# Opening loads cut up and reordered, first low parts on GpSimd, spread product moved into the second gate product

## The reference

```python
def _rmsnorm(x, gain):
    xf = x.astype(jnp.float32)
    y = xf * lax.rsqrt(jnp.mean(xf * xf, axis=-1, keepdims=True) + RMS_EPS)
    return (y * gain.astype(jnp.float32)).astype(x.dtype)
...
    for l in range(DEPTH):
        x = x + 0.5 * swiglu(rmsnorm(x, ffn1_norm[l]), ffn1_w_gate[l], ffn1_w_up[l], ffn1_w_down[l])
```

## Time and profile before

| | us |
|---|---|
| median of 3 runs | 1238.55 (1238.48, 1238.55, 1239.64) |
| span of the profiled execution | 1237.2 |
| PE busy | 1220.2 |
| GpSimd busy | 777.1 |
| ScalarE busy | 617.8 |
| VectorE busy | 538.6 |

### The profile page before, as it was taken

How to read it: one execution, slowest core, us unless ns; L and a number is a source line. 1 busy time by engine, 2 the same in 40 slices (tenths; PEclk the granted TensorE clock), 3 DMA queues, 4 the chain that set the end, 5 groups by cost and what they waited for, 6 DMA issues and landing times.

```text
span 1237.2 us, 23376 instructions
## 1 busy us (share of the span) xinstructions
PE 1220.2 (99%) x9764; PEld 1067.4 (86%) x9764; DVE 538.6 (44%) x821; ACT 617.8 (50%) x812; POOL 777.1 (63%) x195
## 2 busy tenths in 40 slices
PE   8999999999999999999999999999999999999998
PEld 7888887888988888899898888888888998888887
DVE  4232234655333233342523332358968645432233
ACT  7454443445554444585555444464422455644442
POOL 3988880253388888766379888833035425788884
PEclk9999999999999999999999999999999999999999
DMA  7655554243255555554235555532440023455551
GB/s 300 215 186 200 178 195 147 104 172 138 101 189 198 191 198 179 202 194 140 100 137 206 202 183 190 200 139 103 158 167 20 4 105 132 175 205 185 188 202 70
DMA packets 30588, 200.97 MB, mean 162 GB/s; under 512 B 3376, under 2 KB 5296, under 8 KB 6832
## 3 DMA queue, kind: packets, MB, share of 16 engines
q1 hardware_dynamic: 27776, 195.59, 44.0%
q10 hardware_dynamic: 2736, 4.26, 1.0%
HBM read 197.75 MB, written 2.10 MB: 162 GB/s over the span
## 4 chain that ended last, share of the span: by engine, by line
PE 92%; DVE 4%; ACT 1%; issue 1%; POOL 1%; DMA 1%; SPq 0%; POOLq 0%; DVEq 0%
PE psum L351 25%; PE psum L353 13%; PE psum L342 10%; PE psum L344 10%; PE psum L343 10%; PE psum L984 6%; PE psum L997 3%; POOL wlo L3305 1%; PE psum L2822 1%; PE psum L339 1%; PE psum L340 1%; PE psum L341 1%; PE psum L2955 1%; PE psum L2971 1%; PE psum L2841 1%
## 5 line engine op out<-in xcount | busy, mean ns | idle before, releaser
L3305 POOL TENSOR_TENSOR wlo<-raw,whi 128x2048 fp32r<-128x2048 f32 x161 | 741.1, 4609 | 356.2 <-ACT whi L312 308.8
L351 PE MATMUL psum<-f_both,whi 128*128 128x512 f32 x1408 | 492.2, 393 | 1.5 <-DVE wlo L697 1.5
L312 ACT ACTIVATE whi<-raw 128x2048 fp32r<-128x2048 f32 x160 | 306.3, 1915 | 221.7 <-PE psum L353 169.4
L353 PE MATMUL psum<-f_both,wlo 128*128 128x256 f32 x1408 | 393.7, 280 | 0.0
L351 PEld LDWEIGHTS psum<-f_both,whi 128*128 128x128 f32 x1408 | 264.4, 188 | 60.2 <-DVE wlo L697 2.1
L353 PEld LDWEIGHTS psum<-f_both,wlo 128*128 128x128 f32 x1408 | 264.6, 188 | 1.5
L342 PE MATMUL psum<-whi,ahi 128*128 128x512 f32 x352 | 137.4, 390 | 0.3 <-POOL wlo L3305 0.3
L344 PE MATMUL psum<-whi,alo 128*128 128x512 f32 x352 | 137.0, 389 | 0.0
L343 PE MATMUL psum<-wlo,ahi 128*128 128x512 f32 x352 | 137.0, 389 | 0.0
L907 DVE TENSOR_TENSOR psum<-psum,arena 128x512 f32<-128x512 f32 x43 | 30.1, 699 | 241.8 <-ACT arena L623 241.7
L923 DVE TENSOR_TENSOR alo<-arena,ahi 128x512 fp32r<-128x512 f32 x44 | 95.2, 2164 | 31.7 <-ACT ahi L856 31.7
(11 more groups left out here) (416 smaller groups left out, 1532.3 us busy)
## 6 DMA issues: line engine op xcount, KB each, us to landing
raw<-stream SPq DMA_DIRECT2D x182, 1024.0 KB, 4.8
con<-consts SPq DMA_DIRECT2D x1, 1376.0 KB, 14.1
x<-x_in SPq DMA_DIRECT2D x1, 1024.0 KB, 5.0
raw<-stream SPq DMA_DIRECT2D x2, 512.0 KB, 6.9
kept_x<-x ACTq DMA_DIRECT2D x1, 1024.0 KB, 3.9
x<-kept_x ACTq DMA_DIRECT2D x1, 1024.0 KB, 4.7
out<-x SPq DMA_DIRECT2D x4, 256.0 KB, 2.0
arena<-gm_w_s ACTq DMA_DIRECT2D x1, 512.0 KB
```

The lines of the kernel that those rows point to most:

```text
L312: nc.scalar.activation(whi[:, slot, :], raw[:, c % RAW, :], ACT.Copy).then_inc(high_made, 1)
L351: nc.tensor.matmul(psum[:, bank, :].rearrange("p (a n) -> p a n", a=2), whi[w], f_both[:, :, k, :], start=k == 0, stop=False, skip_group_c ...
L353: return nc.tensor.matmul(psum[:, bank, 0:TOK], wlo[w], f_hi[:, k, :], start=False, stop=k == KT - 1, skip_group_check=True)
L3305: nc.gpsimd.tensor_tensor(part(wlo[:, slot, :]), part(raw[:, c % RAW, :]), part(whi[:, slot, :]).bitcast(F32), ALU.subtract)\
```

## The change

It changes five things in the opening.

- Loads, all on SP: identity; x columns 0 to 255; vectors; chunk 0 columns 0 to 511; x 256 to 511; chunk 0 columns 512 to 1023; x 512 to 1023; the rest of chunk 0; chunks 1 and 2; masks. Each piece of x and of chunk 0 has its own semaphore, and each `turn_piece` waits for its part only.
- GpSimd makes the four low pieces of chunk 0 (128x512), VectorE only those of chunk 1.
- ScalarE makes chunk 2's high part in two halves, GpSimd its low part in two halves.
- The idle product after the transposes is gone.
- `spread_scale` no longer stands between up 0 and gate 1, but within gate 1, between its j=0 and j=1 tiles.

Some semaphores elsewhere are merged or renamed, with the awaited values raised to fit. The core of the diff:

```diff
-        def ffn_columns(slot, banks, wait=None):
+        def ffn_columns(slot, banks, wait=None, between=None):
             for j in range(2):
+                if between and j == 1:
+                    between()
                 for k in range(KT):
...
             else:
-                eng.wait_ge(S["x_loaded"], 16)
                 for c in range(2):
                     for j in range(4):
                         if c == 0:
                             high_piece(j)
-                        if (c, j) == (0, 0):
-                            eng.wait_ge(s("raw_left"), 16)
+                        if (c, j) in ((0, 0), (0, 1)):
+                            eng.wait_ge(first_part_loaded[j], 16)
                         if (c, j) in ((0, 2), (1, 0)):
                             eng.wait_ge(raw_loaded[c], 16)
...
-                highs.next = 2
-                highs.upto(2)
+                eng.wait_ge(raw_loaded[2], 16)
+                for j in range(2):
+                    cols = slice(j * 1024, j * 1024 + 1024)
+                    ins = nc.scalar.activation(whi[:, 2, cols], raw[:, 2, cols], ACT.Copy)
+                    ins.then_inc(s("first_high") if j == 0 else high_made, 1)
+                highs.next = 3
                 for j in range(4):
                     square(j)
...
-            def first_low(c, j):
+            def first_up_low(j):
                 cols = slice(j * 512, j * 512 + 512)
-                eng.wait_ge(s("first_high"), 4 * c + j + 1)
-                nc.vector.tensor_tensor(wlo[:, c, cols], raw[:, c, cols], whi[:, c, cols].bitcast(F32), ALU.subtract)\
-                    .then_inc(s("first_low"), 1)
+                eng.wait_ge(s("first_high"), 4 + j + 1)
+                nc.vector.tensor_tensor(wlo[:, 1, cols], raw[:, 1, cols], whi[:, 1, cols].bitcast(F32), ALU.subtract)\
+                    .then_inc(s("first_up_low"), 1)
                 if j == 3:
-                    eng.wait_ge(s("first_low"), 4 * c + 4)
+                    eng.wait_ge(s("first_up_low"), 4)
+                    eng.wait_ge(low_made, 1)
                     nc.vector.tensor_copy(stat[:, 58:59], stat[:, 62:63]).then_inc(low_made, 1)
...
                 else:
                     low_piece(j)
-                    first_low(0, j)
...
             else:
-                eng.wait_ge(S["x_loaded"], 16)
+                eng.wait_ge(x_part_loaded[min(j, 2)], 16)
...
-                eng.wait_ge(S["const_loaded"], 32)
+                eng.wait_ge(s("ident_loaded"), 16)
                 for j in range(4):
                     turn_piece(eng, n, stage, j)
-                idle_products(1)
...
                 if stage == 0:
-                    eng.wait_ge(s("first_low"), k // 2 + 1)
+                    eng.wait_ge(s("first_gate_low"), k // 2 + 1)
...
-                ffn_columns(1, UP_BANKS, wait=lambda k: eng.wait_ge(s("first_low"), 4 + k // 2 + 1)).then_inc(chunk_used, 1)
-                spread_scale(eng, n, 4)
-            step("gate", c0 + 2, 1)
+                ffn_columns(1, UP_BANKS, wait=lambda k: eng.wait_ge(s("first_up_low"), k // 2 + 1)).then_inc(chunk_used, 1)
+            step("gate", c0 + 2, 1, between=None if stage else lambda: spread_scale(eng, n, 4))
...
-            sp.dma_start(x[:, :, :], x_in.rearrange("(m p) d -> p m d", p=P)).then_inc(S["x_loaded"], 16)
-            sp.dma_start(con[:, 0:P], consts[:, 0:P]).then_inc(S["const_loaded"], 16)
-            sp.dma_start(vec[:, :], vectors).then_inc(S["const_loaded"], 16)
-            sp.dma_start(raw[:, 0, 0:1024], stream[0][:, 0:1024]).then_inc(s("raw_left"), 16)
-            sp.dma_start(raw[:, 0, 1024:CHUNK_COLS], stream[0][:, 1024:CHUNK_COLS]).then_inc(raw_loaded[0], 16)
+            x_rows = x_in.rearrange("(m p) d -> p m d", p=P)
+            sp.dma_start(con[:, 0:P], consts[:, 0:P]).then_inc(s("ident_loaded"), 16)
+            for part, (cols, loaded) in enumerate(zip(X_PARTS, x_part_loaded)):
+                sp.dma_start(x[:, :, cols], x_rows[:, :, cols]).then_inc(loaded, 16)
+                if part == 0:
+                    sp.dma_start(vec[:, :], vectors).then_inc(S["const_loaded"], 16)
+                w_cols = slice(2 * cols.start, 2 * cols.stop)
+                sp.dma_start(raw[:, 0, w_cols], stream[0][:, w_cols]).then_inc(raw_loaded[0] if part == 2 else first_part_loaded[part], 16)
...
+            for j in range(4):
+                cols = slice(j * 512, j * 512 + 512)
+                pool.wait_ge(s("first_high"), j + 1)
+                nc.gpsimd.tensor_tensor(wlo[:, 0, cols], raw[:, 0, cols], whi[:, 0, cols].bitcast(F32), ALU.subtract)\
+                    .then_inc(s("first_gate_low"), 1)
+            pool.wait_ge(s("first_gate_low"), 4)
+            nc.gpsimd.tensor_copy(stat[:, 57:58], stat[:, 62:63]).then_inc(low_made, 1)
+            pool.wait_ge(s("first_high"), 9)
+            nc.gpsimd.tensor_tensor(wlo[:, 2, 0:1024], raw[:, 2, 0:1024], whi[:, 2, 0:1024].bitcast(F32), ALU.subtract)\
+                .then_inc(s("first_gate_low"), 1)
             pool.wait_ge(low_made, 2)
+            pool.wait_ge(high_made, 1)
+            pool.wait_ge(s("first_gate_low"), 5)
+            nc.gpsimd.tensor_tensor(wlo[:, 2, 1024:CHUNK_COLS], raw[:, 2, 1024:CHUNK_COLS], whi[:, 2, 1024:CHUNK_COLS].bitcast(F32),
+                                    ALU.subtract).then_inc(low_made, 1)
```

More of the change, by code:

```diff
@@ L274, in build @@
         raw_loaded = [sem(f"raw_loaded{i}") for i in range(RAW)]
-        for n in ("high_made", "low_made", "chunk_used", "const_loaded", "x_loaded", "stored",
+        X_PARTS = (slice(0, 256), slice(256, 512), slice(512, 1024))
+        x_part_loaded = [sem(f"x_part_loaded{i}") for i in range(3)]
+        first_part_loaded = [sem(f"first_part_loaded{i}") for i in range(2)]
+        for n in ("high_made", "low_made", "chunk_used", "const_loaded", "stored",
                   "x_ready", "rms_squares", "rms_root", "rms_scale", "rows_scaled", "turned", "h_high", "h_low",
@@ L714, in pieces_vector @@
                 for j in range(4):
-                    first_low(1, j)
+                    first_up_low(j)
                 eng.wait_ge(chunk_used, CH[("gate", 0, 0)] + 1)
@@ L767, in ffn_tensor, with step @@
             turned_next = f < 2
-            def step(kind, c, g, start=False, stop=False, i=None):
+            def step(kind, c, g, start=False, stop=False, i=None, between=None):
                 b, slot, more = g % 2, c % SPLIT, lambda v, k: v if i is None else v + k * i
@@ L777, in step @@
                         eng.wait_ge(s("ffn_scaled"), GROUPS * f + more(g, 2))
-                    ffn_columns(slot, GATE_BANKS).then_inc(chunk_used, 1)
+                    ffn_columns(slot, GATE_BANKS, between=between).then_inc(chunk_used, 1)
                 if kind == "up":
@@ L1483, in layer_normed @@
             def layer_normed():
-                eng.wait_ge(s("m1_lnroot"), 1)
+                eng.wait_ge(s("m1_root"), 2)
                 steps(nc.vector.reciprocal(lnr[:, 2:4], lnr[:, 0:2]))
@@ L1513, in mix1_vector @@
                 .then_inc(s("m1_osum"), 1)
-            eng.wait_ge(s("m1_oroot"), 1)
+            eng.wait_ge(s("m1_root"), 3)
             steps(nc.vector.reciprocal(orr, ort))
@@ L2808, in rwkv_vector @@
             y_low(3)
-            eng.wait_ge(s("x_back"), 16)
+            eng.wait_ge(s("x_kept"), 32)
         def rwkv_tensor(eng, st):
@@ L3310, in lows_ffn @@
                 for c in range(c0, c0 + 3):
-                    if c >= 2:
+                    if c >= RAW:
                         low(c)
@@ L3336, in _ @@
             highs = Highs(act_eng)
-            act_eng.wait_ge(S["const_loaded"], 32)
-            act_eng.wait_ge(S["eps_ready"], 5)
+            act_eng.wait_ge(S["const_loaded"], 16)
+            act_eng.wait_ge(S["eps_ready"], 6)
             for k, st in enumerate(STAGES):
@@ L3355, in _ @@
             nc.vector.memset(stat[:, 60:61], 64 * EPS).then_inc(S["eps_ready"], 1)
-            nc.vector.memset(idle, 0.0).then_inc(s("idle_filled"), 1)
+            nc.vector.memset(idle, 0.0).then_inc(S["eps_ready"], 1)
             nc.vector.memset(stat[:, 59:60], 64e-5).then_inc(S["eps_ready"], 1)
-            dve.wait_ge(S["x_loaded"], 16)
-            dve.wait_ge(S["const_loaded"], 32)
+            dve.wait_ge(S["const_loaded"], 16)
             column = lambda name: vec[:, VEC_AT[name]:VEC_AT[name] + 8]
```

12 lines of the change are left out of this document (6 added, 6 removed).

## The result

The changed kernel took 1245.21 us (median of five runs, 1242.90 to 1246.69); the kernel before took 1239.64 us in the same call. The ratio is 1.0047, with an interval of 1.0036 to 1.0058. So it is slower by more than the bound of 0.2%, and 4 us above the top of the predicted range. The median of before is taken over five runs, one of which took 6933.97 us; without that one it is 1239.10, and the loss is 6.1 us instead of 5.6. An interval this narrow can't contain that run. The profiled execution has a span of 1242.9 us, 5.7 above that of before, and a mean granted clock of 0.997. In later runs of the kernel before, a run's time was its own span plus 1.8 us (in after's five runs plus 1.9 to 2.3); the 1.35 us of the prediction is the distance between one execution's span and the median of three runs, and by that offset the execution with the median was not the profiled one.

A forecast was written before the change was run, and what follows sets the result against it. TensorE was taken as the bound, the time moving only with the first down product's start. Spread inside gate 1 moved that from 34.9 to 35.9 us, +1.0, added to the 1238.55 us median: 1239.5 us, range 1237.9 to 1241.2.

The forecast's parts named there:

- What bounds the kernel: TensorE, busy 1220.2 of 1237.2 us; the time moves as the first down product's start (34.88 us) moves, by nothing else.
- Part 1: Loads in pieces: x's last half lands at 8.7 us, chunk 2 at 15.0 (bounds 14.3 and 16.5).
- the rule that I had set aside: Loads of at least 1 MiB advised; by it the 1.76 MB in front would take 7.3 instead of 5.2 us.
- Part 2: First gate product starts at 9.7 us, GpSimd's 1.3 us pieces keep up, removed idle product costs nothing.
- Part 3: Chunk 2 in halves costs ScalarE 0.09 us more; GpSimd's halves end at 18.5 and 20.9 us, in time for gate 1.
- The collision that was charged nothing: VectorE's low pieces of chunk 1 meeting GpSimd on SBUF reads: charged nothing, 1.3 us at most if they collide.
- Part 4: Spread product inside the second gate product: spread 1.7 us later, silu 1.0 us later, first down product +1.0 us.
- the wait for `ffn_sum`: Before the second gate product, TensorE, free at 20.8 us, waits 0.7 us for VectorE's sum.
- the exchange: TensorE's stall before the spread (about 1.3 us) becomes 0.7 us at `ffn_sum`, 0.6 at up, 1.8 at down 0.
- late loads: Rival: extra issues paid in full, chunk 2 lands at 16.5 us, +2.5 us in all, 1241.0 us; chance 0.10.
- the falling clock: Rival: longer rests in the opening lower TensorE's clock, +1.0 + 0.4 to 4.4 us, 1240.0 to 1243 us; chance 0.07.

The follow-up runs named there:

- r12: r9 with chunk 2 whole, as in the kernel before, instead of in halves: 1238.70 us, ratio 0.9999 to the kernel before.
- r6: Changed kernel with x cut by tokens (whole rows of 4 KB), not by columns, same sizes and places in the queue: 1244.57 us, ratio 1.0040.
- r10: Changed kernel with the same eleven loads in another order, x's three pieces first, then chunk 0's three: 1242.39 us, ratio 1.0027.
- r11: Kernel before with only chunk 0's low parts on GpSimd and chunk 2 in halves; old loads, idle product and spread place: 1238.90 us, ratio 0.9999.
- r1: Changed kernel with the old loads (x whole, chunk 0 in two halves): 1242.8 us, ratio 1.0037.
- r2: Kernel before with the new loads alone, their waits and the merged semaphores; old idle product, spread and lows stay: 1240.76 us, ratio 1.0015.
- r5: Changed kernel with eight idle products between the groups of transposes: 1242.57 us, ratio 1.0027.
- r9: Kernel before with chunk 2 in halves, right half before squares, spread after four gate 1 tiles, chunk 4's high part before `ahi`, three idle products: 1238.99 us.
- r7: r1 (changed kernel with the old loads) with five idle products after the transposes: 1241.09 us, ratio 1.0014 to the kernel before.
- r4: Kernel before with the spread product inside gate 1, nothing else: 1241.16 us, ratio 1.0017.
- r8: Changed kernel with x in one load behind the identity, chunk 0 still in three pieces: 1241.53 us, ratio 1.0021.

## Why the prediction was wrong

**What bounds the kernel** held for this change: the shift at the first down product, 5.4 us, is the shift at the end of the first FFN and, to 0.3 us, of the span. "And by nothing else" went too far: r12's gain of 0.8 us there did not reach the end.

**Part 1, the landings, is the step that failed first.** I took x's last half at 8.7 us and chunk 2 at 15.0, with 16.5 as the bound; they landed at 11.5 and 17.8. My ground was that the earlier trace rows showed a full queue and the earlier trace rows many small packets at 365 GB/s. What the earlier trace rows say of packet size was even right: in the same microsecond r6 has large packets and 188 GB/s, after small ones and 181. But they are rows of a queue in the old order, and say nothing of how fast it moves when pieces of x and of the weights alternate. In after the queue moved 213 and 222 GB/s over 5 us. At before's 360 and 300 the same 5 us would have moved 0.56 MB more, which is 1.3 us at the later 430 GB/s. SP, too, was held up: two of its issues took 2.36 us, up to 1.3 for one, instead of 0.45 each. Here the rule that I had set aside, that of the Trainium skill ("DMA: Bandwidth & Descriptors", Bandwidth), was nearer: the estimate by it was 2.1 us, the measured delay is 2.8. Single executions divide it: 1.5 for the alternation and 1.3 for the cutting (r10), with at most 0.8 for the packet size (r6), each uncertain by the scatter of the landings, up to 1 us. What in the queue makes alternation slow, and whether SP's hold-up is its cause or its effect, stays open; no run tells them apart.

**Part 2, the first gate product at 9.7**: it started at 13.21, 11.5 + 1.7 for the transposes, which is the late landing and the slow clock together. That GpSimd's 1.3 us pieces keep up was right: PE has no wait between the tiles of the first product in after or r11. What the removed idle product costs alone is not shown. With the old loads, r1, without it, loses the clock in five runs of six, while r11, with it and the old place of the spread, is no slower than before; but with the new loads it does not save the clock (r2), while eight of them do (r5, worth 2.2 us).

**Part 3, halves and GpSimd's lows**: 0.0 measured (r11), as predicted, though the first product there started at 10.92 and not early: with x whole, GpSimd's slower piece moves it by 0.8 us, which the wait at the spread covers. The collision that was charged nothing was absent in after, but r9 showed its price when the times shift: 1.04 us on PE.

**Part 4, the inner spread**: predicted +1.0 at down 0, measured 1.2 there (r7 minus r11) and 1.8 in the time. The mechanism was as told, eight tiles ahead of the spread against 0.75 us of slack at the table load. In after itself the wait for `ffn_sum` was absent, since the slow first products ended up 0 only at about 26.3, 2 us after L726; r5 showed it (0.67 us, predicted 0.7). The two other waits of the exchange came in after, in other sizes: 0.81 us in the second up product for L926 (predicted 0.6) and 1.25 at down 0 (predicted 1.8). The other half microsecond of the time arises behind the first FFN: r7 ends it 1.2 us after r11 (192.4 against 191.2) and writes its last `x` 2.0 us after it (1236.4 against 1234.4). By what, I could not show: the later stages scatter by 0.5 to 0.7 us between executions.

**The rivals.** Two of them came true together, and I had priced each alone: late loads, at a chance of 10% and capped at 16.5 where 17.8 came, and the falling clock, at 7%. The cap was made from the 1.5 us of extra issuing, not from what a slower queue would do, and the clock's chance was set on a longest rest "of about 2 us"; the late x stretched the rests to 1.63 and 2.49 us. New loads alone bring the clock down (r2), so the two should have stood as one case as well: +1.0 for the spread, +1.5 for the landing at the cap, and the +0.4 to +4.4 that the prediction had for the clock (measured: 2.2); on 1238.55 us that is 1241.5 to 1245.5, and the result of 1245.21 lies near its upper end. With the landing as it came, 1.3 us later still, it is 1242.8 to 1246.8; this is said with the result known.

## What to carry to other kernels

Order the first loads by use, but keep each source's pieces together and few: here cutting two tensors up and alternating their pieces delayed what stood behind them by 2.8 us, more than early arrival could give. When a load moves later, look at once at what the matrix engine does meanwhile: a rest longer than any that the kernel had before can cost its clock, and a handful of idle products there is cheap insurance (five in r7, eight in r5; no run below 1.000). And work put in front of a small product on which a long chain hangs delays that chain by up to its full length; weigh it against the slack that the chain really has.

## What the hardware showed that I had not expected

- The length of the last rest does not decide by itself whether the clock falls. Before rested for up to 1.5 us and stayed at 1.000 in most runs; in profiled executions, rests ahead of the first product of 2.36 us (r10) and 2.37 (r4) went with a fall to 0.50 (1.2 GHz), while 2.48 in r8 and 3.00 in r1 kept 1.00. It differs from run to run: seven of r4's eleven timed runs show 1.000, and only one of r1's six. The Trainium skill ("TensorE: Matmul & The Clock Gate", What's actually happening) names two states, 1.2 and 2.4 GHz, and calls the slow matmuls at a kernel's start variable from run to run. The trace agrees: 0.50 from 11 to 17 us in after, with matmuls at 0.63 to 0.78 us that take 0.39 to 0.50 at 1.00, values between only where it changes, and clocks from 0.998 to 1.000 among the timed runs of one kernel (r4).
- Loads waiting in a queue do not make a fixed rate: with the DMA share at 0.81 and 0.82 the changed kernel moved 213 and 222 GB/s, where before moved 360 at 0.91 and 300 at 1.02, and both, from 10 to 15 us, 426 to 441 at 1.01 to 1.05.
- Beside GpSimd a VectorE instruction can take far longer than the 1.3 us that the prediction had as its worst case: in r12 a 0.69 us instruction (the one that is L923 in the earlier trace rows) lasted from 28.49 until 33.45, longer than one of GpSimd's 4.6 us chunks, while GpSimd worked without a pause.

```profile
28.49 4.96 DVE L926 TENSOR_TENSOR alo<-arena,ahi 128x512 fp32r<-128x512 f32 x1 [0.80 <-ACT ahi L857]
```
